# Mixers of a two-layer decoder: projection tiles cut into units between the small products, and another order of branch tiles

## The chip, the cores and the metric

The kernel runs on one core of a Trainium2 chip. The time is that of the device for one launch, in microseconds (us), the median of several executions. Engines are named as the profile does: PE (TensorE, matrix products), DVE (VectorE), ACT (ScalarE), POOL (GpSimd) and SP (SyncE, which issues most transfers). PE has a clock of two levels, 1.2 and 2.4 GHz; the profile shows the share that was granted.

## The reference, cut to what matters

One inference step of a decoder with two layers, on 288 tokens: a prompt of 256 and 8 sequences of 4 sampled tokens. What the change touches is the first part of each layer, the token mixers:

```
z = u @ w_in                     # u: normalised input, 288 x 1024
a = GLA(z[...]), b = RetNet(z[...]), c = gated DeltaNet(z[...]), d = Mamba-2 SSD(z[...])
br = stack(a, b, c, d)           # each 288 x 512
proj = einsum('blnv,nvd->blnd', br, w_branch)
gates = sigmoid(mg)              # mg: the last 4 x 1024 columns of z
out = sum(gates * proj, over n) @ w_out
```

DeltaNet and SSD first run a causal convolution of width 4 over their columns. DeltaNet (GDN) also inverts a triangular matrix of 128 x 128 per head and block, in seven doubling levels. After the mixers come a SwiGLU (layer 0) or experts (layer 1) and a gate with a per-layer embedding. The states of all mixers are outputs too.

## The kernel before

All weights come through one stream of tiles of 128 x 1024 floats (512 KB) into a ring of five slots (RING), in the order that `tile_table` writes down. A tile is one of:
- `z`: a block of 128 columns of the input projection, for one mixer n. GLA, RetNet and GDN have 12 each, SSD has 10.
- `mg`: a block of the gate columns; 8 for each mixer.
- `br`: two blocks of the branch projection of mixer n, for which the final output of that mixer is needed; 4 for each mixer.

`z` and `mg` tiles are *projection tiles*. They are computed in a split form: ACT rounds the tile to a high part (`high`, L1346), DVE subtracts to get the low part (`low`, L1688), and PE sums three products (high x high, high x low, low x high, L715 to L717) for each of the 8 blocks of 128 rows: 24 products of 288 columns. The split tiles lie in three buffers (HELD), so the split of a tile waits until the tile three before it is done. A projection tile's ring slot is free when its low part is made. A *branch tile* isn't split: PE reads it from the ring (L762, 2 x 4 products, 16 records in the trace), and its slot is free when PE is done. SP waits for exactly these events, in the order of the stream, before it issues the transfer into a slot (`plain`, L677).

PE writes tile t to bank t % 2 (a branch tile to both). ACT takes a projection tile out of its bank: a `z` tile is copied to memory (L1374, L1375, L1378), an `mg` tile goes through a tanh (L1370). DVE takes a branch tile (`branch_tile`): (tanh + 1) times the product, for each of two banks (L1712), and from the second mixer on it is added to the sum (L1715). Before a tile is written, PE waits in `bank_is_free` until the tile that had the bank was taken.

The mixers run one after the other: `gla`, `ret`, `gdn`, `ssd`. Their own products are small and wait for each other through DVE, ACT and POOL. To fill PE, each mixer's order of work has numbered slots, and `SLOTS[n]` says how many tiles of the stream are issued in each; `fill(L, n, s)` issues them. The same call stands in ACT's and DVE's programs: ACT takes the tiles of the slot and makes the high parts that fall due (`highs`), DVE makes the low parts (`lows`) and takes the branch tiles. So the slots also set what ACT and DVE do ahead of and behind the mixer's own work. Each engine runs its own list in order. While mixer n runs, `z` tiles of mixer n + 1, `mg` tiles and the `br` tiles of mixer n - 1 are issued.

Places in a mixer that matter here:
- `core`: scores (L785), and for two heads at a time `outputs`: three products a head (L891 to L893), and for each of 8 sequences one product per head with the state as weights and 4 columns (L896).
- `out_sums` (L926, L929) behind a wait for ACT's squares, and `states` (L946, L950, L954), which waits for the masks that POOL makes.
- GDN and SSD start with `conv`: for each block of channels DVE makes four operations (L1908 to L1914), ACT a tanh (L1484), DVE two operations that finish it (L1896, L1898), and both fill one slot with it. On ACT the slot comes ahead of the tanh; on DVE it comes behind the finish. PE doesn't wait between slots 0 to 4.
- behind it GDN normalises queries and keys (reciprocal L2026, products L2028, L2029), then come the transposes (L842, L847) and the decays of the heads (L861 to L864).
- in GDN's inversion a level is 8 products (16 records, L1062), a copy by ACT (L1536), 16 products (L1069, L1071) and two subtractions by DVE (L2074, L2075), on which the next level waits.

Of the kernel before, what the change touches and what calls it, by code (L numbers as in the profile page):

```python
# [23 lines left out]
P = 128  # L24
# [4 lines left out]
TOK = SEQ + SAMP  # L29
# [165 lines left out]
def tile_table():  # L195

    out = []
    for L in range(DEPTH):
        def z(n):
            return [("z", L, n, b) for b in range(ZBLOCKS[n])]  # L200

        def mg(n):
            return [("mg", L, n, b) for b in range(KD)]

        def br(n):
            return [("br", L, n, b) for b in range(4)]

        out += z(0)
        out += z(1) + mg(0)
        out += br(0) + z(2) + mg(1)  # L210
        out += br(1) + z(3) + mg(2)
        out += br(2) + mg(3)
        out += br(3)
        out += [("out", L, 0, b) for b in range(KD)]
        if L % 2 == 0:
            for b in range(NF):
                out += [("gate", L, 0, b), ("up", L, 0, b)]
            out += [("down", L, 0, b) for b in range(NF)]
# [36 lines left out]
def tile_at(j, m, i):  # L255
# [1 line left out]
    return 2 * FIRST[j] + m * GROUPS[j] + i  # L257

SLOTS = [
# [5 lines left out]
]  # L265
NSLOT = [len(x) for x in SLOTS]


def fill_tiles(L):
    out = []  # L270
    for n in range(4):
        mine = [x for x in PLAIN if x[1] == L and ((x[0] == "z" and x[2] == n + 1) or (x[0] == "mg" and x[2] == n) or
                                                  (x[0] == "br" and x[2] == n - 1))]
# [30 lines left out]
def build(nc, io):  # L304
    ctx = ExitStack()
    with ctx:
# [391 lines left out]
        def _(pe):  # L698
            mm = nc.tensor.matmul

            def weights(x):
# [2 lines left out]
                pe.wait_ge(slot_in[t % RING], 16 * (t // RING + 1))  # L704
                return [ring[:, (t % RING) * TILE + P * i:(t % RING) * TILE + P * i + P] for i in range(8)]

            def product(out, x, uh, ul, norm_k=None):

                t = T_OF[x]
                q = Q_OF[t]  # L710
                pe.wait_ge(tile_low, q + 1)
                hi, lo = [[y[:, q % HELD, P * i:P * i + P] for i in range(KD)] for y in (t_high, t_low)]
                if norm_k is None:
                    for k in range(KD):
                        mm(out, hi[k], uh[:, k, :], start=k == 0, stop=False)  # L715
                        mm(out, hi[k], ul[:, k, :], start=False, stop=False)  # L716
                        last = mm(out, lo[k], uh[:, k, :], start=False, stop=k == KD - 1)  # L717
                    return last
                for k in range(KD):
# [18 lines left out]
            def stream_tile(x):  # L738
# [29 lines left out]
                            last = mm(bank(M + o)[:, 0:TOK], w[2 * o + k], ple_in[:, k, :], start=k == 0, stop=k == 1)  # L768
                last.then_inc(tile_done, 1)

            def fill(L, n, s):
                for x in FILL[L][n][s]:
                    stream_tile(x)

            def norm(k):
                for i in range(KD):
# [12 lines left out]
            def prep(L):  # L789
                pe.wait_ge(small_in[L], 16 * 5)  # L790
                for k in range(KD):
                    mm(bank(M)[0:16, 0:TOK], wsm[:, k, 0:16], u[:, k, :], start=k == 0, stop=k == KD - 1)
                for b, (t0, nt) in enumerate(TB):
                    for k in range(KD):
                        last = mm(bank(M + 1)[0:nt, 16 * b:16 * b + 16], u[:, k, t0:t0 + nt], wsm[:, k, 16:32],
                                  start=k == 0, stop=k == KD - 1)
                last.then_inc(small_ps, 1)
                pe.wait_ge(glr_ready, L + 1)
                for b, (t0, nt) in enumerate(TB):
                    last = mm(bank(M + 2 + b // 2)[0:nt, 256 * (b % 2):256 * (b % 2) + 256],  # L800
                              glrt[0:17, t0:t0 + nt], wgk[0:17, :], start=True, stop=True)
                last.then_inc(gk_ps, 1)
                for b in range(4, ZBLOCKS[0]):
                    stream_tile(("z", L, 0, b))
                pe.wait_ge(logd_ready, L + 1)

# [62 lines left out]
            def core(L, n, slot):  # L869
# [3 lines left out]
                def outputs(h0):  # L873
# [20 lines left out]
                    for b in range(NSEQ):  # L894
                        for i, (kr, pair, o, p, v) in enumerate(two):
                            last = mm(o[:, 256 + 4 * b:260 + 4 * b], st_of(n)[kr, pair, b, :],  # L896
                                      qg[kr, pair, 4 * b:4 * b + 4], start=False, stop=True, skip_group_check=True)
                            if b == NSEQ - 1:
                                last.then_inc(o_ps, 1)

                for hh in range(HEADS[n]):
                    gh = L * NHEAD + HBASE[n] + hh
                    if n != GLA:
                        kT, qT = qk_of(n, hh)
                        if hh < 2:
# [8 lines left out]
                        outputs(hh - 1)  # L914
                    fill(L, n, slot + hh)
                if n != GLA:
                    outputs(HEADS[n] - 2)

            def out_sums(L, n):
# [12 lines left out]
            def states(L, n):  # L932

                m, dv = 4 * L + n, DV[n]
                pe.wait_ge(ort_ready, m + 1)
                pe.wait_ge(o_taken, L * NHEAD + HBASE[n] + HEADS[n])
                for h0 in range(0, HEADS[n], 2):
                    gh = L * NHEAD + HBASE[n] + h0
                    two = []
# [12 lines left out]
                    for b in range(NSEQ):  # L952
                        for r, pair, kc, v, mk in two:
                            last = mm(bank(M + 2 * pair + b // 4)[r, dv * (b % 4):dv * (b % 4) + dv],  # L954
                                      mk[:, 64 * b:64 * b + 64], v[0:32, 2], start=True, stop=True)
                            if b == NSEQ - 1:
                                last.then_inc(masked_used, 1)

            def gla(L):
                m = 4 * L  # L960
# [41 lines left out]
                fill(L, GLA, 15)  # L1002
                out_sums(L, GLA)
                fill(L, GLA, 16)
                states(L, GLA)
                fill(L, GLA, 17)

            def gdn(L):
# [48 lines left out]
                for lv in range(7):  # L1057
# [4 lines left out]
                        last = mm(bank(M + g // 4)[:, 128 * (g % 4):128 * (g % 4) + 128], msk[:, g // 2, g % 2, :],  # L1062
                                  xm[:, g // 2, g % 2, :], start=True, stop=True)
                    last.then_inc(p_ps, 1)
                    fill(L, GDN, 16 + 2 * lv)
                    pe.wait_ge(p_ready, 7 * L + lv + 1)
                    for g in range(8):
                        c = slice(128 * (g % 4), 128 * (g % 4) + 128)
# [11 lines left out]
                last.then_inc(vn0_ps, 1)  # L1080
                pe.wait_ge(kbg_ready, L + 1)
                pe.wait_ge(state_in, 16 * (4 * L + GDN + 1))
                for b in range(NSEQ):
                    for hh in range(4):
                        r = slice(64 * (hh % 2), 64 * (hh % 2) + 64)
                        last = mm(bank(M + 1 + 4 * (hh % 2))[:, 32 * (hh // 2) + 4 * b:32 * (hh // 2) + 4 * b + 4], st_of(GDN)[r, hh // 2, b, :],
# [25 lines left out]
                fill(L, GDN, 37)  # L1112
                out_sums(L, GDN)
                fill(L, GDN, 38)
                states(L, GDN)
                for s in range(39, NSLOT[GDN]):
                    fill(L, GDN, s)

            def ret(L):
# [11 lines left out]
                fill(L, RET, 6)  # L1131
                out_sums(L, RET)
                fill(L, RET, 7)
                states(L, RET)
                for s in range(8, NSLOT[RET]):
                    fill(L, RET, s)

# [1463 lines left out]
```

## Time and profile before

| | |
|---|---|
| median of 3 runs | 2736.98 us (2736.95 to 2749.7) |
| profiled execution | 2750.4 us |
| its span, first to last instruction | 2748.3 us |
| mean granted clock of PE | 0.914 |
| busy share of the span | PE 90%, PE weight loads 77%, DVE 59%, ACT 39%, POOL 7% |
| mixers of layer 0 from GLA's transposes to the last branch tile | 82.9 to 714.1 us |
| the same of layer 1 | 1090.6 to 1707.4 us |

Busy shares are those of one execution. A product's duration in the rows is longer than the step from one start to the next, since products overlap in the array; for a run of products the steps count. A granted clock of 1.0 is the full level and 0.5 the half one, and a figure between is a mean over time. "idle before <-releaser" is how long the engine stood still ahead of the instruction, and the instruction of which engine let it go.

### The profile page before, as it was taken

The page shows a single profiled execution, that of the slowest core. Times are in us where ns is not written, and L with a number is a line of the kernel's source. Part 1 is how long each engine was busy: PE and PEld are TensorE (multiplying, and loading weights), DVE is VectorE, ACT ScalarE, POOL GpSimd, SP SyncE. Part 2 cuts the span into 40 slices and gives each one's busy share as a digit, 9 for nine tenths or more (in the row PEclk, how much of TensorE's full clock was granted, in tenths as well). Part 3 has the DMA queues.
Part 4 walks back from the last instruction along what each step waited for, and adds up shares of the span by engine and source line. Part 5 has one row for each costly group of instructions (what it writes and reads, how often), then busy time and mean ns, then how long its engine had stood idle before and what let it go on. Part 6 is the DMA issues. An engine that isn't in the chain of part 4 may idle for free.

```text
span 2748.3 us, 38217 instructions
## 1 busy us (share of the span) xinstructions
PE 2462.7 (90%) x14436; PEld 2124.5 (77%) x14436; DVE 1628.5 (59%) x2112; ACT 1074.4 (39%) x1450; POOL 178.8 (7%) x247
## 2 busy tenths in 40 slices
PE   8899868868999989889778879899999999999996
PEld 7788758857699978779678766678878778787786
DVE  4453554264366463544553443387887878778785
ACT  3322321112033343324221121166766667567563
POOL 0210101111000000211011201000000000000000
PEclk8889879778899999999889688799999999999999
DMA  5224321021345432323311122288988889889871
GB/s 192 93 82 141 117 74 50 31 97 39 137 146 166 164 129 93 105 103 115 125 54 47 59 70 72 90 309 301 333 294 317 303 300 331 294 299 321 299 282 74
DMA packets 122566, 456.43 MB, mean 166 GB/s; under 512 B 14056, under 2 KB 14474, under 8 KB 120018
## 3 DMA queue, kind: packets, MB, share of 16 engines
q1 hardware_dynamic: 118818, 432.66, 44.6%
q0 software_dynamic: 3632, 22.12, 2.2%
q8 instruction: 86, 1.41, 0.2%
q14 instruction: 30, 0.25, 0.0%
HBM read 443.72 MB, written 11.00 MB: 165 GB/s over the span
## 4 chain that ended last, share of the span: by engine, by line
PE 77%; DVE 11%; issue 5%; ACT 4%; DMA 1%; POOL 1%; DVEq 0%; SPq 0%; ACTq 0%; POOLq 0%
PE ps L715 9%; PE ps L717 8%; PE ps L716 8%; PE ps L762 5%; DVE weights_low L2220 4%; PE ps L1265 4%; PE ps L1267 3%; PE ps L1266 3%; PE ps L1287 3%; PE ps L1288 3%; PE ps L1289 3%; PE ps L1238 3%; PE ps L756 2%; PE ps L896 2%; DMA ring<-in_stream 1%
## 5 line engine op out<-in xcount | busy, mean ns | idle before, releaser
L715 PE MATMUL ps<-u_high,tiles_high 128*128 128x288 f32 x1688 | 535.1, 317 | 2.6 <-DVE arena L1712 2.6
L716 PE MATMUL ps<-u_low,tiles_high 128*128 128x288 f32 x1688 | 521.3, 309 | 0.0
L717 PE MATMUL ps<-u_high,tiles_low 128*128 128x288 f32 x1688 | 519.1, 307 | 0.0
L1688 DVE TENSOR_TENSOR tiles_low<-ring,tiles_high 128x1024 fp32r<-128x1024 f32 x238 | 291.7, 1229 | 268.7 <-ACT tiles_high L1346 267.6
L715 PEld LDWEIGHTS ps<-u_high,tiles_high 128*128 128x128 f32 x1688 | 340.8, 202 | 12.7 <-issue 6.7
L1346 ACT ACTIVATE tiles_high<-ring 128x1024 fp32r<-128x1024 f32 x238 | 250.7, 1054 | 245.9 <-DMA ring<-in_stream 155.9
L716 PEld LDWEIGHTS ps<-u_low,tiles_high 128*128 128x128 f32 x1688 | 341.0, 202 | 0.6
L717 PEld LDWEIGHTS ps<-u_high,tiles_low 128*128 128x128 f32 x1688 | 340.3, 202 | 0.0
L2220 DVE TENSOR_TENSOR weights_low<-expert_ring,weights_high 128x1024 fp32r<-128x1024 f32 x288 | 334.3, 1217 | 4.9 <-ACT weights_high L1597 2.2
L1265 PE MATMUL ps<-weights_high,u_high 128*128 128x512 f32 (+1 forms) x768 | 297.6, 388 | 23.2 <-DVE weights_low L2220 22.6
L2220 DVE TENSOR_TENSOR weights_low<-ring,weights_high 128x1024 fp32r<-128x1024 f32 x240 | 280.1, 1217 | 42.9 <-ACT weights_high L1597 41.8
L1597 ACT ACTIVATE weights_high<-expert_ring 128x1024 fp32r<-128x1024 f32 x288 | 283.3, 1052 | 27.4 <-PE ps L1267 27.4
L1267 PE MATMUL ps<-weights_high,u_low 128*128 128x512 f32 (+1 forms) x768 | 289.1, 376 | 0.0
L1266 PE MATMUL ps<-weights_low,u_high 128*128 128x512 f32 (+1 forms) x768 | 289.0, 376 | 0.0
L1597 ACT ACTIVATE weights_high<-ring 128x1024 fp32r<-128x1024 f32 x240 | 236.4, 1052 | 78.9 <-PE ps L1289 42.2
L762 PE MATMUL ps<-arena,ring 128*128 128x288 f32 x512 | 155.9, 470 | 64.2 <-DVE arena L1712 59.6
L762 PEld LDWEIGHTS ps<-arena,ring 128*128 128x128 f32 x512 | 113.2, 224 | 106.7 <-issue 71.7
L1265 PEld LDWEIGHTS ps<-weights_high,u_high 128*128 128x128 f32 x768 | 144.5, 188 | 59.9 <-DVE weights_low L2220 38.1
L1267 PEld LDWEIGHTS ps<-weights_high,u_low 128*128 128x128 f32 x768 | 144.5, 188 | 23.4
L1266 PEld LDWEIGHTS ps<-weights_low,u_high 128*128 128x128 f32 x768 | 144.8, 188 | 21.7
L1287 PE MATMUL ps<-weights_high,tiles_high 128*128 128x512 f32 x352 | 141.1, 401 | 0.0
L1288 PE MATMUL ps<-weights_low,tiles_high 128*128 128x512 f32 x352 | 139.5, 396 | 0.0
(381 smaller groups left out, 3377.6 us busy)
## 6 DMA issues: line engine op xcount, KB each, us to landing
ring<-in_stream SPq DMA_DIRECT2D x530, 512.0 KB, 4.2
expert_ring<-in_stream SPq DMA_DIRECT2D x288, 512.0 KB, 5.5
arena<-in_state POOLq DMA_DIRECT2D x8, 1024.0 KB, 5.2
state_s<-arena POOLq DMA_DIRECT2D x8, 1024.0 KB, 4.2
const<-in_const SPq DMA_DIRECT2D x1, 2052.5 KB, 12.0
arena<-in_const POOLq DMA_DIRECT2D x2, 832.0 KB, 4.9
h<-in_x SPq DMA_DIRECT2D x1, 1152.0 KB, 5.1
y<-acc POOLq DMA_DIRECT2D x1, 1152.0 KB, 4.4
```

Of the source, the lines that this page charges most:

```text
L715: mm(out, hi[k], uh[:, k, :], start=k == 0, stop=False)
L716: mm(out, hi[k], ul[:, k, :], start=False, stop=False)
L717: last = mm(out, lo[k], uh[:, k, :], start=False, stop=k == KD - 1)
L762: last = mm(bank(o)[:, 0:TOK], w[4 * o + k], src, start=k == 0, stop=k == 3)
L1265: mm(out, xg_high[:, k, :], hi, start=k == 0, stop=False)
L1266: mm(out, xg_high[:, k, :], lo, start=False, stop=False)
L1267: last = mm(out, xg_low[:, k, :], hi, start=False, stop=k == KD - 1)
L1287: mm(out, e_high[:, f, :], hi, start=f == 0, stop=False)
L1346: A(t_high[:, q % HELD, :], ring[:, (t % RING) * TILE:(t % RING + 1) * TILE], ACT.Copy).then_inc(tile_high, 1)
L1597: A(w_high[:, o // 4, o % 4].rearrange("p k c -> p (k c)"), expert_slot(t), ACT.Copy).then_inc(w_high_ready, 1)
L1688: tt(t_low[:, q % HELD, :], ring[:, (t % RING) * TILE:(t % RING + 1) * TILE], t_high[:, q % HELD, :].bitcast(F32), ALU.subtract).then_inc( ...
L2220: tt(lo, expert_slot(t), hi.bitcast(F32), ALU.subtract).then_inc(w_low_ready, 1)
```

## The change

1. `tile_table` has another order: with mixer n's slots no longer go `br` of n - 1, `z` of n + 1 and `mg` of n. The gate tiles of mixer 1 move from RetNet's slots to the start of GDN's, ahead of `br(1)`; those of mixer 2 from GDN's slots to the start of SSD's, ahead of `br(2)`. `MG_STAGE` says which mixer's slots take which gate tiles. RetNet's slots hold 16 tiles instead of 24, GDN's 22 as before, SSD's 20 instead of 12.
2. `SLOTS` is written anew. In GDN's slots 0 to 5, ahead of and in the convolutions, stand the eight gate tiles, in 6 and 7 a branch tile each, in 13 and 17 one each, and then one `z` tile in each level of the inversion from the second on (slots 19 to 29), in 35 and in 37 to 39. In SSD's slots 0 to 7 stands a gate tile each, in 9 to 12 (between the decays of pairs of heads) a branch tile each, and gate tiles in 13, 15, 17, 19, two in 21 and two in 22.
3. On PE a tile can be issued in units: three products of a projection tile, or one product of a branch tile. `begin` waits for the bank and makes the tile the current one, `drip` issues some of its units, and `fill` first issues what is left of it and then the other tiles of the slot. Units stand:
   - in `prep` between the small projections for the token-major gates (L795), with the tile `z` 4 that stood behind the next products before
   - in `outputs`, one unit behind the products of each of the 8 sequences
   - in `states` of GLA, RetNet and GDN, one for every second sequence
   - in GDN's inversion, three units between the first and the second group of products of a level
4. On ACT and DVE only the order of tiles changes, through the tables.

```diff
-        out += br(0) + z(2) + mg(1)
-        out += br(1) + z(3) + mg(2)
-        out += br(2) + mg(3)
+        out += br(0) + z(2)
+        out += mg(1) + br(1) + z(3)
+        out += mg(2) + br(2) + mg(3)
...
 SLOTS = [
-    [2, 2, 2, 1, 1, 1, 1, 0, 1, 0, 1, 1, 1, 1, 1, 1, 1, 2],
-    [3, 2, 2, 3, 3, 2, 2, 2, 2, 3],
-    [1, 0, 1, 1, 0, 1, 0, 2, 0, 1, 0, 0, 2, 1, 0, 1, 0, 1, 0, 1, 0, 1, 0, 1, 0, 1, 1, 0, 0, 0, 1,
-     1, 0, 0, 0, 0, 0, 1, 1, 1, 0],
-    [0, 1, 1, 2, 1, 0, 1, 0, 0, 1, 0, 0, 0, 0, 0, 0, 0, 1, 0, 1, 0, 2, 1],
+    [3, 1, 2, 1, 1, 1, 1, 0, 1, 0, 1, 1, 1, 1, 1, 1, 1, 2],
+    [2, 1, 1, 1, 2, 1, 2, 2, 2, 2],
+    [1, 1, 2, 1, 2, 1, 1, 1, 0, 0, 0, 0, 0, 1, 0, 0] + [0, 1] * 7 + [0, 0, 0, 0, 0, 1, 0, 1, 1, 1, 0],
+    [1, 1, 1, 1, 1, 1, 1, 1, 0, 1, 1, 1, 1, 1, 0, 1, 0, 1, 0, 1, 0, 2, 2],
 ]
+MG_STAGE = [0, 2, 3, 3]
...
+            def product_units(out, x):
+                q = Q_OF[T_OF[x]]
+                pe.wait_ge(tile_low, q + 1)
+                for k in range(KD):
+                    hi, lo = [y[:, q % HELD, P * k:P * k + P] for y in (t_high, t_low)]
+                    mm(out, hi, u_high[:, k, :], start=k == 0, stop=False)
+                    mm(out, hi, u_low[:, k, :], start=False, stop=False)
+                    last = mm(out, lo, u_high[:, k, :], start=False, stop=k == KD - 1)
+                    if k == KD - 1:
+                        last.then_inc(tile_done, 1)
+                    yield
...
+                def begin(self, x):
+                    self.tile = x
+                    t = T_OF[x]
+                    if x[0] == "br":
+                        self.units = branch_units(x)
+                    else:
+                        bank_is_free(t, t % 2)
+                        self.units = product_units(bank(t % 2)[:, 0:TOK], x)
+                def drip(self, count):
+                    for _ in range(count if self.units else 0):
+                        next(self.units, None)
+                def finish(self):
+                    self.drip(9)
+                    done, self.tile, self.units = self.tile, None, None
+                    return done
...
             def fill(L, n, s):
+                begun = tiles.finish()
                 for x in FILL[L][n][s]:
-                    stream_tile(x)
+                    if x != begun:
+                        stream_tile(x)
... in prep
+                tiles.begin(("z", L, 0, 4))
                 for b, (t0, nt) in enumerate(TB):
                     for k in range(KD):
...
+                        if k % 3 == 2:
+                            tiles.drip(1)
+                tiles.finish()
                 pe.wait_ge(glr_ready, L + 1)
... in outputs, behind the two heads' products of a sequence
+                        tiles.drip(1)
... in core
                 for hh in range(HEADS[n]):
+                    begin(L, n, slot + hh)
...
                 if n != GLA:
+                    begin(L, n, slot + HEADS[n])
                     outputs(HEADS[n] - 2)
... in states (slots 17, 39 and 8 of GLA, GDN and RetNet; none for SSD)
+                if slot is not None:
+                    begin(L, n, slot)
...
+                        if b % 2:
+                            tiles.drip(1)
... in the inversion
                     last.then_inc(p_ps, 1)
-                    fill(L, GDN, 16 + 2 * lv)
+                    begin(L, GDN, 17 + 2 * lv)
+                    tiles.drip(3)
                     pe.wait_ge(p_ready, 7 * L + lv + 1)
```

## Rows read from the trace of the kernel before

**Rows 1.** Page, busy us, share of the span and instructions of each engine.
```profile
PE 2462.7 (90%) x14436; PEld 2124.5 (77%) x14436; DVE 1628.5 (59%) x2112; ACT 1074.4 (39%) x1450; POOL 178.8 (7%) x247
```

**Rows 2.** Stretches: window, us, busy by engine, granted clock, DMA share, GB/s.
```profile
210.40:328.50 118.10, 110.00 (x773) 100.88 (x772) 56.24 (x57) 35.15 (x57) 16.89 (x35) 0.94 0.40 135
328.50:388.20 59.70, 30.38 (x121) 23.29 (x119) 35.92 (x59) 14.49 (x22) 0.00 (x0) 0.73 0.20 71
388.20:431.50 43.30, 40.98 (x258) 36.79 (x259) 20.15 (x43) 8.79 (x23) 4.84 (x7) 0.78 0.18 61
431.50:503.40 71.90, 60.28 (x482) 58.78 (x480) 28.33 (x26) 16.64 (x21) 11.04 (x13) 0.98 0.13 45
503.40:569.40 66.00, 62.28 (x421) 56.88 (x422) 27.12 (x28) 10.86 (x16) 10.10 (x8) 0.69 0.09 29
569.40:613.00 43.60, 24.39 (x88) 18.21 (x86) 23.30 (x48) 6.92 (x12) 3.55 (x14) 0.77 0.35 127
613.00:634.00 21.00, 17.83 (x111) 15.67 (x111) 14.72 (x43) 8.04 (x21) 3.08 (x2) 1.00 0.19 65
634.00:696.10 62.10, 55.89 (x364) 39.71 (x364) 21.53 (x30) 12.71 (x20) 10.81 (x10) 0.76 0.08 26
```

**Rows 3.** Stretches again: the mixers of layer 0 and of layer 1.
```profile
82.90:714.10 631.20, 535.00 (x3533) 467.79 (x3533) 298.74 (x419) 150.60 (x252) 86.15 (x116) 0.84 0.24 81
...
1090.60:1707.40 616.80, 521.86 (x3533) 456.38 (x3533) 298.81 (x419) 151.90 (x253) 86.42 (x116) 0.86 0.24 82
```

**Rows 4.** PE's waits in layer 0's mixers: us in total, times, longest.
```profile
PE ps L762 <- DVE arena L1712: 30.5, 4, 9.3
PE ps L842 <- DVE arena L2029: 13.9, 1, 13.9
PE ps L1069 <- ACT arena L1536: 6.7, 6, 1.1
...
PE ps L1062 <- DVE arena L2075: 2.5, 1, 2.5
```

**Rows 5.** Timeline of GDN's convolutions: start, us, instruction, [idle before, releaser].
```profile
328.37 4.04 PE L762 MATMUL ps<-arena,ring 128*128 128x288 f32 x16
339.54 7.11 PE L762 MATMUL ps<-arena,ring 128*128 128x288 f32 x16 [7.13 <-DVE arena L1712]
...
349.92 1.06 ACT L1346 ACTIVATE tiles_high<-ring 128x1024 fp32r<-128x1024 f32 x1 [12.37 <-DMA ring<-in_stream]
...
351.36 0.42 DVE L1896 SCALAR_TENSOR_TENSOR arena<-arena 128x256 f32<-128x256 f32 x1 [5.95 <-ACT arena L1484]
...
353.66 6.88 PE L762 MATMUL ps<-arena,ring 128*128 128x288 f32 x16 [7.01 <-DVE arena L1712]
...
355.18 0.55 DVE L1910 SCALAR_TENSOR_TENSOR arena<-arena,pv 128x312 f32<-128x312 f32 x1
...
379.36 7.35 DVE L2026 RECIPROCAL arena<-arena 128x1152 f32<-128x1152 f32 x1
```

**Rows 6.** Timeline of PE: products in a row, at the half and the full level.
```profile
48.29 0.44 PE L715 MATMUL ps<-u_high,tiles_high 128*128 128x288 f32 x1
48.53 0.44 PE L716 MATMUL ps<-u_low,tiles_high 128*128 128x288 f32 x1
...
286.07 0.30 PE L716 MATMUL ps<-u_low,tiles_high 128*128 128x288 f32 x1
286.20 0.29 PE L717 MATMUL ps<-u_high,tiles_low 128*128 128x288 f32 x1
```

**Rows 7.** Page, the costliest groups: DVE's split of a tile.
```profile
L1688 DVE TENSOR_TENSOR tiles_low<-ring,tiles_high 128x1024 fp32r<-128x1024 f32 x238 | 291.7, 1229 | 268.7 <-ACT tiles_high L1346 267.6
```

**Rows 8.** Timeline of PE: around one pair of RetNet's outputs.
```profile
281.69 0.59 PE L891 MATMUL ps<-arena 128*128 128x256 f32 x2
...
282.76 0.70 PE L891 MATMUL ps<-arena 128*128 128x256 f32 x2
...
285.83 0.40 PE L715 MATMUL ps<-u_high,tiles_high 128*128 128x288 f32 x1
```

More of the change, by code:

```diff
@@ L271, in fill_tiles @@
     for n in range(4):
-        mine = [x for x in PLAIN if x[1] == L and ((x[0] == "z" and x[2] == n + 1) or (x[0] == "mg" and x[2] == n) or
+        mine = [x for x in PLAIN if x[1] == L and ((x[0] == "z" and x[2] == n + 1) or (x[0] == "mg" and MG_STAGE[x[2]] == n) or
                                                   (x[0] == "br" and x[2] == n - 1))]
@@ L705, in weights, with branch_units, __init__ @@
                 return [ring[:, (t % RING) * TILE + P * i:(t % RING) * TILE + P * i + P] for i in range(8)]
+            def product_units(out, x):
[9 more added lines that the diff above has]
+                    yield
+            def branch_units(x):
+                t = T_OF[x]
+                _, L, n, b = x
+                pe.wait_ge(o_final, 4 * L + n + 1)
+                w = weights(x)
+                for o in range(2):
+                    bank_is_free(t, o)
+                    for k in range(4):
+                        last = mm(bank(o)[:, 0:TOK], w[4 * o + k], zblk(n, OUT0[n] + k)[:, 0:TOK], start=k == 0, stop=k == 3)
+                        if k == 3:
+                            last.then_inc((branch_ps, tile_done)[o], 1)
+                        yield
+            class Fill:
+                def __init__(self):
+                    self.tile = self.units = None
+                def begin(self, x):
+                    self.tile = x
+                    t = T_OF[x]
+                    if x[0] == "br":
[10 more added lines that the diff above has]
+                    return done
+            tiles = Fill()
             def product(out, x, uh, ul, norm_k=None):
@@ L769, in stream_tile, with begin @@
                 last.then_inc(tile_done, 1)
+            def begin(L, n, s):
+                if FILL[L][n][s]:
+                    tiles.begin(FILL[L][n][s][0])
             def fill(L, n, s):
+                begun = tiles.finish()
                 for x in FILL[L][n][s]:
-                    stream_tile(x)
+                    if x != begun:
+                        stream_tile(x)
             def norm(k):
@@ L796, in prep @@
                                   start=k == 0, stop=k == KD - 1)
-                last.then_inc(small_ps, 1)
+                        if (b, k) == (2, KD - 1):
+                            last.then_inc(small_ps, 1)
+                        if k % 3 == 2:
+                            tiles.drip(1)
+                tiles.finish()
                 pe.wait_ge(glr_ready, L + 1)
@@ L802, in prep @@
                 last.then_inc(gk_ps, 1)
-                for b in range(4, ZBLOCKS[0]):
+                for b in range(5, ZBLOCKS[0]):
                     stream_tile(("z", L, 0, b))
@@ L930, in out_sums, with states @@
                 last.then_inc(osum_ps, 1)
-            def states(L, n):
+            def states(L, n, slot=None):
                 m, dv = 4 * L + n, DV[n]
@@ L1004, in gla @@
                 fill(L, GLA, 16)
-                states(L, GLA)
+                states(L, GLA, 17)
                 fill(L, GLA, 17)
@@ L1082, in gdn @@
                 pe.wait_ge(state_in, 16 * (4 * L + GDN + 1))
+                begin(L, GDN, 30)
                 for b in range(NSEQ):
+                    tiles.drip(1)
                     for hh in range(4):
@@ L1114, in gdn @@
                 fill(L, GDN, 38)
-                states(L, GDN)
+                states(L, GDN, 39)
                 for s in range(39, NSLOT[GDN]):
@@ L1133, in ret @@
                 fill(L, RET, 7)
-                states(L, RET)
+                states(L, RET, 8)
                 for s in range(8, NSLOT[RET]):
```

## The prediction

> **What bounds the kernel now.** I read the page's busy rows first. TensorE (PE) is busy in 90% of the span [rows 1], so only what shortens PE's own work or fills its idle time counts. Then the stages of the four mixers of layer 0, cut where PE's work changes [rows 2]: RetNet is full (110.0 of 118.1 us), the two stretches in which VectorE (DVE) computes the short convolutions are half empty (30.4 of 59.7 and 24.4 of 43.6), and the stretches with many small products are full but run at a granted clock of 0.69 to 0.78. Layer 1 repeats this: the same stages take 616.8 us against 631.2, with the same instruction count and a clock of 0.86 and 0.84 [rows 3]. I work out one layer and double it; everything outside the mixers is taken as it is. The waits of PE say why the convolution stretches are empty [rows 4]: branch products (L762) wait 30.5 us for DVE to take the branch before (L1712), one transpose waits 13.9 us for the normalised keys (L2029), and in the delta rule's inversion (GDN) six products wait 1.1 us each for ScalarE's (ACT) copy, the last level 2.5 us for DVE's subtraction.
>
> How the long wait comes about is in the timeline of one convolution step [rows 5]. A branch product ends near 346.65 (339.54 + 7.11). Its slot in the ring is then free, the next transfer lands, and ACT, which waited 12.37 us for it, splits that tile at 349.92. Only after that does ACT compute the tanh of the convolution, on which DVE waits 5.95 us until 351.36, and only behind that does DVE take the branch, so that PE's next branch product starts at 353.66. One such turn takes 14.1 us for 4.0 us of products.
>
> **The units of work.** A projection tile is 24 products. At the full level (2.4 GHz) they start 0.133 us apart, 3.2 us a tile; at the half level (1.2 GHz) 0.24 us apart, 5.8 us [rows 6]. A branch tile is 16 records, 4.04 us at the full level and 7.1 at the half [rows 5].
>
> **The change, part by part, in one layer.** Both orders issue 46 projection and 12 branch tiles from RetNet's start on. No product, split or transfer is added or lost; DVE's 1.23 us [rows 7] and ACT's 1.06 us [rows 5] per split go with the tile.
>
> 1. *RetNet, 118.1 us.* Eight gate tiles leave a stretch that PE fills: 8 x 3.2 = -25.6. Its own chain (scores, sums, states) still has 12 tiles beside it, and PE's only waits there are a few us.
> 2. *GDN's convolutions, 59.7 us.* Before: 2 projection and 4 branch tiles. After: 8 and 2. Six of the eight conv steps now turn on projection tiles, whose slot is free once they are split, so ACT doesn't wait for a transfer. Eight tiles 25.6, the sums 2.1, some 7 for splits that DVE reaches late (a conv block is 4 operations of at most 0.55, some 2.1 us, [rows 5]), a branch tile 4.0, the wait for its taking 7.1, the second at the half level 7.1. Then the tail: transfer 3.3 (346.65 to 349.92), split 1.1, tanh, finish, split, branch taking (some 5, a sum of neighbouring rows, my estimate), reciprocal 7.35, two products 1.5. Together 71 to 73: +13. Ends: 54 (-6) if nothing waits beside the tail, 88 (+28) if every tile costs half a turn.
> 3. *To the inversion, 43.3 us.* Five projection tiles leave, one branch tile comes: -16.0 + 4.0; decays and the small inverse then wait some 2 us openly. -10 (ends -13, -5).
> 4. *Inversion, 71.9 us.* Nine products (1.2 us) now stand in the 1.1 us for which PE waits on ACT, and fifteen (2.0) behind the second group. They were the cover of DVE's subtraction, which needs 2.5 us [rows 4]: 0.5 us becomes open per level. Six times -1.1 + 0.5, the last level 2.5 to 0.5: -5.5 (ends -8, 0). One branch tile more fits in.
> 5. *GDN's outputs and states, 66.0 us at 0.69.* That clock means 62% of it, 41 us, at the half level, where a product takes 0.24 instead of 0.133: 18 us lost. The weights products with 4 columns (L896) alone precede such drops. With three 288-column products between every few of them I expect a third back, -6, not all, as the waits ahead of the outputs stay. One tile fewer -3.2; the tile that hid ACT's taking and square now stands ahead of them, +3 of open wait: about -7 (ends -21, +3).
> 6. *SSD's convolutions, 43.6 us.* Four branch tiles go, six projection tiles come. The pace is then DVE's block: 2.1 + finish 0.6 + split 1.2 = 3.9, six times, and 2.6 at the start: 26. -17.5 (ends -20, 0).
> 7. *SSD's transposes and decays, 21.0 us.* Four branch tiles come between the pairs of heads, 16.2 us of products. Each must be taken by DVE (two products and a sum, some 1.6) behind a split that waits for a transfer, but the decay products of the next pair lie beside. +13 (ends +8; +45 if each costs the whole turn of 14.1, less the 11 us of decays beside them).
> 8. *SSD's core, sums and states, 62.1 us at 0.76.* Three tiles more, +9.6; 48% at the half level costs 13 us, of which I count 7 back; the wait for y before the sums grows by 3: +6 (ends -1, +13).
> 9. *The switching.* A projection product behind a small one starts 0.24 instead of 0.133 us ahead of its follower (285.83, 286.07, 286.20 [rows 6, 8]); a small pair behind a projection product takes 0.59 instead of 0.70 [rows 8]. Net some 0.08 us a unit (ends 0 and 0.18), in some 94 units: +7.
> 10. *Start of the layer and GLA.* Three tiles in GLA's first slot look as if they fill its wait (L974), but DVE must first split for the third, which waits for the tile before it, so the wait moves along: 0. The tile among the small projections runs earlier, but its bank is only read by ACT after the logarithms, so the tile that reuses the bank waits: -1. GLA's two cores win the clock in one layer and lose the cover of the square (2 us): 0.
>
> The wait for a free bank now stands ahead of small products, with outputs and states queued behind it on PE, and ACT and DVE after them. It is for a tile two before, which ACT has taken by then in its own order, so I cost it at nothing; if ACT were late, the outputs would start late by one tile, 3.2.
>
> Sum: -25.6 + 13 - 10 - 5.5 - 7 - 17.5 + 13 + 6 + 7 - 1 = -27.6 us a layer, -55 in both. The profiled execution took 2750.4 us (span 2748.3), so it would take 2695; the median before is 2736.98, 13.4 lower, and by it the forecast is **2682 us**.
>
> **A rule against it.** The rows first: over both layers' mixers the granted clock is 0.84 and 0.86 [rows 3], so some 30% of 1248 us pass at the half level, and I count 13 us a layer of that back. "TensorE: Matmul & The Clock Gate" of the Trainium skill (What's actually happening) says that the ramp is under 1% of a typical kernel's span. By it less than 27 us could be won from the clock in all, and the bounds of steps 5 and 8 would lose their lower ends. This trace doesn't agree for this kernel.
> A second one (Step-by-step: what each phase is for, same page) is that PE pulls the next weight load ahead under a running product. By it the switching of step 9 would be a gain rather than a cost. The row on the small pair agrees (0.59 against 0.70), the row on the product behind it does not.
>
> **The rivals.**
> *The clock holds.* If small and large products mixed keep PE at the full level in steps 3, 5 and 8, 19 + 41 + 30 us at the half level end, worth 0.45 each: 40 us instead of the 13 counted. -27 more a layer: 2628. For it: the inversion, products without long pauses, runs at 0.98 [rows 2]. Against: the waits ahead of each core remain.
> *Moved, not hidden.* The convolution stretches may not be held by branch tiles but by the alternation ACT, DVE, PE, which projection tiles need too (take, split, tanh, finish, split). Then step 6 gives nothing (+17.5) and step 2 costs 5 more: +45 in both layers, 2727. For it: every convolution step waits for ACT (5.95). Against: the 12.37 us are a wait for a transfer that only branch slots cause.
> *The turn goes with the branch tile (slower).* Six branch tiles of a layer now stand in GDN's slots 13 and 17 and between SSD's decays. If each drags ACT and DVE through the turn of 14.1 us, step 7 costs 32 more and the two others 10 each: +52 a layer, 2786. It decides, that is over 2751, from 5.8 us more per tile. For it: the same transfer wait stands in ACT's queue ahead of the decays' exponentials. Against: four of them have other PE work beside, and no convolution waits.
>
> **How the numbers follow.** Forecast (2650 to 2713) 0.63, clock 0.12, moved 0.15, slower 0.10. Under 0.5%, 13.7 us, this kernel can't be told from unchanged. Faster: 0.63 + 0.12 and a third of the third case, 0.80; same 0.10; slower 0.10. The range leaves out the far half of the first rival and the slower one: 2640 to 2732.
>
> **What would show it.** L762's wait for L1712 falls from 30 us to some 10 a layer (2, 6). RetNet's stretch is near 92 us; L842's wait for L2029 grows to about 18 (2). L1069's wait for L1536 is gone and L1062 waits 0.5 per level (4). SSD's convolutions take about 26 us, its decays about 25 to 34 with transposes (6, 7). A clock over 0.9 in the output stretches would say that I took too little from it; a split (L1346) waiting over 5 us for a transfer between SSD's decays that I took too little for step 7. Wrong altogether if the two layers' mixers together are not shorter by 30 to 80 us.

## The result, and the profile after

The changed kernel takes 2807.64 us (median of 4 runs, 2802.55 to 2808.91) against 2736.97 beside it: the ratio is 1.024, with an interval of 1.021 to 1.027. It is slower by 2.4%, where 2682 was forecast. Its profiled execution took 2806.45 us, with a span of 2804.7 and a mean granted clock of 0.908. Two of kernel 4's ten executions below, at 3961 and 7926 us, were disturbed, and its 2742.7 is the median of the other eight.

The page's busy rows of the changed kernel, against [rows 1]:

```profile
PE 2540.4 (91%) x14436; PEld 2145.0 (76%) x14436; DVE 1631.4 (58%) x2112; ACT 1071.8 (38%) x1450; POOL 178.9 (6%) x247
```

DVE and ACT do the same work. PE, with the same 14436 records, is busy 78 us longer: the loss is inside PE's own work, not in waits. The stretches of layer 0 in the changed kernel, cut at the same events as [rows 2] (window, us, busy of PE, PEld, DVE, ACT, POOL, granted clock, DMA share, GB/s), and then the mixers of both layers, against [rows 3]:

```profile
211.30:320.40 109.10, 98.84 (x578) 82.64 (x577) 43.61 (x44) 24.67 (x42) 15.17 (x32) 0.84 0.30 107
320.40:395.60 75.20, 42.74 (x237) 37.88 (x235) 41.62 (x66) 21.47 (x31) 0.62 (x4) 0.79 0.22 77
395.60:434.10 38.50, 31.30 (x154) 23.84 (x154) 18.28 (x43) 3.25 (x11) 4.83 (x7) 0.68 0.04 14
434.10:503.40 69.30, 65.96 (x496) 62.28 (x496) 27.65 (x29) 14.61 (x24) 9.99 (x13) 0.96 0.17 62
503.40:580.50 77.10, 70.15 (x396) 55.65 (x397) 25.61 (x26) 11.05 (x17) 10.09 (x6) 0.64 0.09 28
580.50:605.80 25.30, 21.41 (x145) 20.35 (x144) 23.88 (x43) 11.94 (x20) 5.99 (x16) 0.95 0.60 202
605.80:640.80 35.00, 33.23 (x175) 27.73 (x175) 23.75 (x58) 8.78 (x22) 2.05 (x2) 1.00 0.25 78
640.80:714.60 73.80, 66.51 (x436) 47.03 (x436) 22.33 (x32) 16.78 (x26) 10.78 (x10) 0.89 0.18 63
83.60:733.80 650.20, 562.91 (x3533) 469.67 (x3533) 301.36 (x421) 149.32 (x252) 86.66 (x116) 0.84 0.23 78
1108.40:1764.00 655.60, 570.70 (x3533) 474.85 (x3533) 300.42 (x421) 150.85 (x254) 86.00 (x116) 0.84 0.23 78
```

RetNet gave up eight tiles, 25.6 us of products, and is only 9 us shorter at a clock of 0.84 (0.94 before). GDN's outputs and states are 11 us longer, not 7 shorter. Both layers' mixers together are 57.8 us longer (19.0 and 38.8), where the forecast had called itself wrong altogether unless they were 30 to 80 shorter. SSD's convolutions (25.3) and its transposes with decays (35.0) are where the forecast put them (26 and 34).

PE's waits in layer 0 of the changed kernel, against [rows 4]. L818 is the branch product, L911 the transposes, L998 SSD's sums behind ACT's squares, L713 a unit's product, L1138 the inversion's first products:

```profile
PE ps L911 <- DVE arena L2108: 18.3, 1, 18.3
...
PE ps L818 <- DVE arena L1791: 7.2, 1, 7.2
PE ps L998 <- ACT arena L1534: 5.6, 1, 5.6
...
PE ps L713 <- DVE tiles_low L1767: 3.2, 1, 3.2
...
PE ps L1138 <- DVE arena L2154: 2.7, 5, 0.5
```

The waits went as forecast: branch products 30.5 to 7.2, the keys 18.3, the inversion's six waits for ACT's copy gone, 0.5 open per level. And yet the layer is longer.

What a unit costs is in PE's timeline of the changed kernel, in RetNet's outputs of layer 1 at the full level and in GDN's outputs of layer 0 at the half one. L965 x4 are the four small products of a sequence, with 4 columns each, L713 to L715 the unit:

```profile
1274.41 0.39 PE L965 MATMUL ps<-arena 64*128 64x4 f32 x4
1274.73 0.40 PE L713 MATMUL ps<-u_high,tiles_high 128*128 128x288 f32 x1
1274.97 0.29 PE L714 MATMUL ps<-u_low,tiles_high 128*128 128x288 f32 x1
1275.10 0.29 PE L715 MATMUL ps<-u_high,tiles_low 128*128 128x288 f32 x1
1275.32 0.39 PE L965 MATMUL ps<-arena 64*128 64x4 f32 x4
...
532.04 0.61 PE L713 MATMUL ps<-u_high,tiles_high 128*128 128x288 f32 x1
...
533.58 0.61 PE L713 MATMUL ps<-u_high,tiles_high 128*128 128x288 f32 x1
```

A cycle of four small records and a unit takes 0.91 us at the full level (1274.41 to 1275.32) and 1.54 at the half (532.04 to 533.58). The same work unmixed stands in the third kernel below (new order, units in the inversion alone):

```profile
252.05 1.95 PE L965 MATMUL ps<-arena 64*128 64x4 f32 x32
253.93 0.40 PE L772 MATMUL ps<-u_high,tiles_high 128*128 128x288 f32 x1
...
501.61 3.58 PE L965 MATMUL ps<-arena 64*128 64x4 f32 x32
505.12 0.61 PE L772 MATMUL ps<-u_high,tiles_high 128*128 128x288 f32 x1
```

32 small records take 1.88 us from start to start, 0.235 for four, or 3.51 and 0.44 at the half level; a unit in a row of products takes 0.40 or 0.72 [rows 6]. So a unit between small products costs 0.91 - 0.64 = 0.27 us at the full level, and 1.54 - 1.16 = 0.38 at the half. The forecast had 0.08. SSD's products on 64 rows and 64 columns pay the same: the cycle is 0.81 (660.07 to 660.88), four of them unmixed take 0.13 (kernel 3, 32 from 623.48 to 624.51), which leaves 0.28.

```profile
660.07 0.28 PE L965 MATMUL ps<-arena 64*64 64x4 f32 x4
...
660.88 0.28 PE L965 MATMUL ps<-arena 64*64 64x4 f32 x4
```
```profile
623.48 1.10 PE L965 MATMUL ps<-arena 64*64 64x4 f32 x32
624.51 0.40 PE L772 MATMUL ps<-u_high,tiles_high 128*128 128x288 f32 x1
```

### The profile page after: what moved, and what is told of

Read it like the earlier page. It is cut to its first block, busy times and chain, and to the rows that moved or that the text cites. A ratio compares the mean times of both kernels' runs of the same rounds, so it can differ in the third digit from the quotient of the medians.

```text
span 2804.7 us, 38220 instructions
## 1 busy us (share of the span) xinstructions
PE 2540.4 (91%) x14436; PEld 2145.0 (76%) x14436; DVE 1631.4 (58%) x2112; ACT 1071.8 (38%) x1450; POOL 178.9 (6%) x247
## 4 chain that ended last, share of the span: by engine, by line
PE 75%; DVE 13%; issue 5%; ACT 4%; POOL 1%; DMA 1%; DVEq 0%; SPq 0%; ACTq 0%; POOLq 0%
PE ps L771 5%; PE ps L773 5%; PE ps L772 5%; PE ps L818 4%; DVE weights_low L2299 4%; PE ps L1344 4%; PE ps L713 3%; PE ps L1346 3%; PE ps L1345 3%; PE ps L1366 3%; PE ps L1367 3%; PE ps L1368 3%; PE ps L1317 3%; PE ps L812 2%; PE ps L965 2%
## 5 line engine op out<-in xcount | busy, mean ns | idle before, releaser
L771 PE MATMUL ps<-u_high,tiles_high 128*128 128x288 f32 x1288 | 401.6, 312 | 20.3 <-DVE tiles_low L1767 17.1
L772 PE MATMUL ps<-u_low,tiles_high 128*128 128x288 f32 x1288 | 393.4, 305 | 0.0
L773 PE MATMUL ps<-u_high,tiles_low 128*128 128x288 f32 x1288 | 391.6, 304 | 0.0
L1676 ACT ACTIVATE weights_high<-expert_ring 128x1024 fp32r<-128x1024 f32 x288 | 283.3, 1051 | 27.6 <-PE ps L1346 27.6
L771 PEld LDWEIGHTS ps<-u_high,tiles_high 128*128 128x128 f32 x1288 | 256.3, 199 | 31.3 <-issue 23.6
L772 PEld LDWEIGHTS ps<-u_low,tiles_high 128*128 128x128 f32 x1288 | 255.9, 199 | 0.7
L773 PEld LDWEIGHTS ps<-u_high,tiles_low 128*128 128x128 f32 x1288 | 255.4, 198 | 0.0
L713 PE MATMUL ps<-u_high,tiles_high 128*128 128x288 f32 x400 | 158.5, 396 | 6.3 <-DVE tiles_low L1767 6.3
L1368 PE MATMUL ps<-weights_high,tiles_low 128*128 128x512 f32 x352 | 139.5, 396 | 0.0
```

The lines of the kernel that those rows point to most:

```text
L713: mm(out, hi, u_high[:, k, :], start=k == 0, stop=False)
L1676: A(w_high[:, o // 4, o % 4].rearrange("p k c -> p (k c)"), expert_slot(t), ACT.Copy).then_inc(w_high_ready, 1)
```

## The experiments

| kernel | us | ratio to before, interval |
|---|---|---|
| changed | 2807.6 | 1.021 to 1.027 |
| 1 new order, no units | 2705.5 | 0.980 to 0.991 |
| 2 old order, all units | 2855.1 | 1.037 to 1.047 |
| 3 new order, units in the inversion | 2701.4 | 0.979 to 0.989 |
| 4 all units but those of the outputs | 2742.7 | 0.997 to 1.003 |
| 5 small products on all rows | 2814.9 | 1.024 to 1.030 |
| 6 lumps of four units | 2720.2 | 0.992 to 0.996 |
| 7 old order, units in the inversion | 2728.5 | 0.994 to 0.998 |
| 8 as 3, branch tiles of GDN later | 2650.1 | 0.964 to 0.969 |
| 9 as 8, gate tiles left in place | 2642.9 | 0.965 to 0.970 |
| 10 changed kernel with the slots of 8 | 2761.1 | 1.007 to 1.011 |
| 11 as 8, one gate tile later too | 2640.3 | 0.964 to 0.967 |
| 12 as 8, lumps in GLA and GDN | 2654.4 | 0.969 to 0.972 |

**1 to 4: units or order.** `MIX` says where `begin` acts; where it doesn't, the tile is issued whole in its slot.

```
+MIX = ()                # 2: all places, and the old tile_table and SLOTS; 3: ("inv",); 4: all but "out"
-                if FILL[L][n][s]:
+                if where in MIX and FILL[L][n][s]:
```

> The new order and slots, with every tile issued whole in its slot as before the change. Theory A (the units cost): the traces of before and after show one cycle of small products and a unit at the full level in 0.91 us, against 0.64 for the same work unmixed, +0.27 us; some 110 units a layer stand among small products, 59 us in both layers, and the stretches of outputs stay at the half level with them. So without units the time is 2807 - 59 = 2748, down to 2720 if the clock comes back too. Theory B (the order costs: gate tiles put into the convolutions, branch tiles between SSD's decays): the time stays at 2790 or more.

> The old order and slots (one tile of the inversion moved by half a level, from slot 26 to 27), with units in all the places of the change. Theory A: 2737 + 59 for switching, less some 5 to 10 for the inversion, more if the clock stays low: 2785 to 2815. Theory B: within 10 us of 2737.

> The new order, with units in the inversion alone. Theory A: 3 to 5 us a layer under the new order alone (forecast step 4 gave 5.5, the stretch of the changed kernel showed 2.7 to 3.6): 2712 to 2742. Theory B: 2785 or more.

> The changed kernel without the units in the four outputs (80 of 110 a layer); those in the start, in the states and in the inversion stay. Theory A: 2807 - 160 x 0.27 = 2764, down to 2745 if the clock comes back in the outputs. Theory B: 2795 or more.

Theory A (the units cost) holds and B (the order costs) falls: without units the new order is 1.5% faster than before, and units under the old order alone cost 117 us (the old slots put 64 of them a layer in the outputs instead of 80, and 8 among GDN's products of keys and states). The units cost more than the expectations had: kernels 1 and 3 came out below their ranges, kernel 2 above. From kernel 3 to the changed one 106 us are lost in 2 x 110 units outside the inversion, 0.48 each: 65 in the 160 units of the outputs, 41 in the other 60. Kernel 3's whole tiles follow such small products 13 times a layer and pay a change there too, so 194 changes were added, not 220; at 0.27 to 0.38 each they explain 52 to 74.

SSD's core shows the change almost alone, as its clock hardly moves: the stretch in kernel 3, in the changed kernel, and in kernel 6 below.

```profile
601.70:640.50 38.80, 35.96 (x333) 31.60 (x333) 15.49 (x26) 11.07 (x19) 4.66 (x4) 0.96 0.25 92
```
```profile
640.80:689.00 48.20, 42.59 (x332) 33.21 (x332) 15.52 (x26) 10.91 (x18) 4.64 (x4) 0.96 0.20 74
```
```profile
611.20:652.90 41.70, 37.19 (x332) 32.12 (x332) 15.51 (x27) 10.96 (x18) 4.65 (x4) 0.94 0.24 87
```

PE goes 4, 32 and 8 times from 4-column products to a projection product there: 9.4 us for 28 times more (0.34 each), 6.5 us back for 24 fewer (0.27).

Elsewhere the clock and waits come on top. They show in RetNet's sums and states of layer 1, the same 162 records of PE in both kernels: the window of kernel 3, that of kernel 4, and PE's timeline of kernel 4 inside it:

```profile
1242.30:1265.80 23.50, 20.81 (x162) 19.31 (x161) 16.39 (x8) 6.75 (x11) 4.28 (x4) 0.78 0.33 118
```
```profile
1262.70:1293.40 30.70, 26.05 (x162) 20.40 (x161) 12.28 (x7) 6.75 (x11) 2.04 (x2) 0.72 0.21 69
```
```profile
1271.89 0.65 PE L1029 MATMUL ps<-arena 32*64 32x128 f32 x8
1277.11 0.61 PE L714 MATMUL ps<-u_high,tiles_high 128*128 128x288 f32 x1 [4.57 <-DVE tiles_low L1768]
1277.52 0.44 PE L715 MATMUL ps<-u_low,tiles_high 128*128 128x288 f32 x1
```

The mixed order takes 7.2 us more for eight units. The first unit waits 4.57 us for DVE's split, with the states queued behind it (kernel 3 waits 2.7 there, for POOL's masks). Behind the pause PE is at the half level (a product lasts 0.44, as in [rows 6]) and stays there until the last unit; in kernel 3 the same products stand in one row behind the states.

**5: why a switch costs.** SSD's small products are 64 x 64, RetNet's 64 x 128, and both pay 0.27 to 0.28, so half the columns of the array make no difference here.

```
-                        two.append((slice(64 * half, 64 * half + 64), pair,
+                        two.append((slice(64 * half, 64 * half + 64) if n == SSD else slice(0, P), pair,
```

> The changed kernel, where the small products of GLA's, RetNet's and GDN's outputs use all 128 rows of the array instead of 64 (the sum then runs over two heads' rows, so these outputs are not the reference's; SSD's stay as they are). A cycle of four small records and a unit takes 0.907 us in the changed kernel, 0.27 more than unmixed. Theory A1 (the price comes from changing the shape of the tile in the array, 64 rows against 128): the cycle falls to 0.64 to 0.70, and the time by some 96 x 0.25 = 24 us to 2785. Theory A2 (any change between a small and a projection product costs this): the cycle stays at 0.88 or more, the time at 2800 to 2815.

The cycle fell to 0.84 or 0.85 at the full level, between the two theories, and the time did not fall (2814.9). What happened is in the weight loads: RetNet's outputs in the changed kernel (L965), and the same in this one (L966).

```profile
1274.97 0.19 PEld L715 LDWEIGHTS ps<-u_high,tiles_low 128*128 128x128 f32 x1
1275.32 0.30 PEld L965 LDWEIGHTS ps<-arena 64*128 64x128 f32 x4 [0.16 <-issue]
```
```profile
1277.46 0.19 PEld L716 LDWEIGHTS ps<-u_high,tiles_low 128*128 128x128 f32 x1
1277.59 0.54 PEld L966 LDWEIGHTS ps<-arena 128*128 128x128 f32 x4
```

On all rows the small load starts 0.13 us behind the load before it, while the last large product runs, and the cycle has nothing left over: 0.40 for the unit and four loads at 0.11 are 0.84. On 64 rows the load starts 0.35 us behind, only with its own product. So the loads speak for A1's mechanism, and its number was missed: I had let the small records keep the 0.06 that they take on 64 rows, while on all rows they take 0.11. At the half level nothing is won: the cycle is 1.57 (below) against 1.54.

```profile
1280.28 0.59 PE L714 MATMUL ps<-u_high,tiles_high 128*128 128x288 f32 x1
...
1281.85 0.59 PE L714 MATMUL ps<-u_high,tiles_high 128*128 128x288 f32 x1
```

No run has these small products on all rows and unmixed. That 0.11 is their own price is read from the loads in the cycle alone, so the cause of the 0.27 is in this last step argued, not shown. "TensorEngine Tiling (Array Packing)" of the Trainium skill (Key Properties) says that a change of tiling mode drains the engine. The loads fit that, at 0.27 us for a change there and back.

**6: the number of switches.**

```
-                        tiles.drip(1)
+                        if b % 4 == 3:
+                            tiles.drip(4)       # in states: drip(2)
```

> The changed kernel with twelve products (four units) behind every fourth sequence of the outputs instead of three behind each, and six products behind every fourth in the states. The same work stands at the same places, with 32 switches a layer there instead of 104. Theory A (each switch costs 0.27): 2 x 72 x 0.27 = 39 us less, 2768, and lower if a longer run of products lets the clock rise. If the place of the tile costs, and not the number of switches (rival C: outputs finished later by a whole tile's time, 3.2 us each in 12 places a layer): it stays at 2795 or more.

2720: 87 us for 144 switches fewer, 0.6 each, with the same tiles in the same places. Rival C (the place of the tile costs) falls. That is more than the change itself, which SSD's core above has at 0.27. What the rest is stays open: the mean clock rose from 0.908 to 0.923, but of layer 0's stretches GLA went from 127.7 to 116.7 us at 0.88 and then 0.93, and GDN's outputs from 76.2 to 65.5 at an unchanged 0.64.

**7: the inversion alone.** Only `MIX = ("inv",)` with the old order (the tile of slot 26 in 27).

> The old order with units in the inversion alone. By step 4 of the forecast 5.5 us a layer (bounds 0 and 8): 2726. With both old order and units everywhere the inversion took 66.4 us against 71.8, 5.4 less, which says the same; under the new order, with a branch tile more in it, the gain was 3.7. Rival: the gain was noise of the clock, 2732 or more.

2728.5, and the inversion takes 66.4 us in both layers (71.9 before [rows 2]): 5.4, as step 4 said. Its products and the units both use all 128 rows. Over both layers that would be 11 us, and the time fell by 8.2.

**8 to 12: the order.** GDN's slots 0 to 15 in the changed kernel, and in kernels 8, 9 and 11 (10 and 12 have those of 8; 12 lets units into GLA's and GDN's outputs, with 6's edit):

```
-[1, 1, 2, 1, 2, 1, 1, 1, 0, 0, 0, 0, 0, 1, 0, 0]   # changed kernel
+[1, 1, 2, 1, 1, 1, 1, 0, 0, 1, 0, 0, 1, 1, 0, 0]   # 8
+[1, 1, 2, 1, 2, 1, 0, 0, 0, 1, 0, 0, 1, 1, 0, 0]   # 9
+[1, 1, 1, 1, 1, 1, 1, 0, 0, 1, 1, 0, 1, 1, 0, 0]   # 11
```

> The new order with units in the inversion alone (2701), with the tiles of GDN's slots 4 to 17 moved later: one gate tile from slot 4 to 5 and on to 6, and the two branch tiles of slots 6 and 7 to slots 9 and 12, behind the transposes. The stretch from GDN's transposes to the inversion runs at 0.63 there, at 0.86 in layer 1 of the kernel before, which had five projection tiles in it. Theory D (without tiles of its own this stretch falls to the half level): with two branch tiles more (8.1 us at the full level) it takes about as long as now, 41 us, at 0.8, while the convolutions lose a branch turn of 10: 2685. Rival: the small products set the clock there whatever stands between, and DVE is late with two more branch tiles: 2700 or more.

> As the kernel with the branch tiles moved later (2650), but all eight gate tiles stay in GDN's slots 0 to 5 (1, 1, 2, 1, 2, 1) and only the two branch tiles go from slots 6 and 7 to 9 and 12. Theory F (the two branch tiles in the last convolution steps cost a turn each, which the forecast priced at 4.0 + 7.1 + 7.1): nearly the whole gain stays, 2645 to 2660. Rival: the gain came from one gate tile less ahead of the fifth step, 2685 or more.

> The changed kernel with all its units, and only the slots of GDN's gate and branch tiles as in the kernel that took 2650. If the price of the units and that of the two branch tiles are independent: 2807 - 51 = 2756, within 8. If the two share their loss of clock: 2770 or more, or 2740 or less.

> As the kernel that took 2650, with gate tiles one in each slot 0 to 6 and the eighth in slot 9, behind the transposes, and the branch tiles in 10, 12, 13 and 17. VectorE sets the pace in the convolutions (PE waits 3.7 us for a split), so one split fewer there makes them 1.2 us shorter, the tile's 3.2 us of products go to a stretch at 0.88: between 2645 and 2655 if the tile only moves, 2640 or less if it also fills the small inverse's waits there (2.1 us a layer) and keeps the clock up.

> As the kernel that took 2650, with twelve products behind every fourth sequence in GLA's and GDN's outputs alone. In the kernel with such lumps everywhere GLA took 2 to 3 us a layer less and GDN's outputs 2.4 less in layer 1, 3.1 more in layer 0. Theory A (few switches cost little, and long runs of products raise the clock where it had fallen): 2640 to 2648. Rival: the difference was chance of the clock, 2648 to 2655.

Kernel 8 gave 51 us where 16 were expected. Kernel 9 shows that it was the two branch tiles (F; 58 us). Kernel 10 falls 46.5 under the changed one: the two prices are independent within some 5 us. Kernel 11 is 10 us under 8 and level with 9. The gain that kernel 6 had let me expect for 12 didn't come: it is 4 us slower than 8. DVE's and ACT's timeline in layer 0 of kernel 3, at the last convolution step, and then DVE's of kernel 9:

```profile
352.68 1.06 ACT L1425 ACTIVATE tiles_high<-ring 128x1024 fp32r<-128x1024 f32 x1 [8.92 <-DMA ring<-in_stream]
...
355.61 0.43 DVE L1975 SCALAR_TENSOR_TENSOR arena<-arena 128x256 f32<-128x256 f32 x1 [11.04 <-ACT arena L1563]
...
358.96 7.35 DVE L2105 RECIPROCAL arena<-arena 128x1152 f32<-128x1152 f32 x1
```
```profile
335.64 0.43 DVE L1975 SCALAR_TENSOR_TENSOR arena<-arena 128x256 f32<-128x256 f32 x1 [1.55 <-ACT arena L1563]
335.98 0.19 DVE L1977 SCALAR_TENSOR_TENSOR arena<-arena 128x32 f32<-128x32 f32 x1
336.20 7.35 DVE L2105 RECIPROCAL arena<-arena 128x1152 f32<-128x1152 f32 x1
```

Behind a branch tile ACT waits 8.92 us for the transfer into its slot, and the tanh stands behind that; with the branch tiles past the transposes DVE waits 1.55 for it instead of 11.04. The stretches of layer 0 from RetNet's start to the transposes, and from there to the inversion, in kernel 3 and then in kernel 9:

```profile
200.50:367.90 167.40, 127.08 (x812) 113.72 (x811) 86.51 (x108) 46.40 (x73) 16.27 (x34) 0.87 0.30 101
367.90:408.90 41.00, 33.77 (x155) 25.48 (x155) 18.32 (x42) 3.25 (x11) 4.85 (x7) 0.62 0.04 14
```
```profile
197.60:345.10 147.50, 116.57 (x781) 106.13 (x779) 80.93 (x100) 44.27 (x71) 16.71 (x35) 0.88 0.32 110
345.10:382.00 36.90, 31.64 (x186) 24.46 (x186) 22.77 (x50) 5.36 (x13) 5.21 (x7) 0.87 0.13 44
```

The two tiles leave 19.9 us behind, and where they go the stretch is 4.1 us shorter with 31 records more, for its clock rises from 0.62 to 0.87. These 24 us are not all: the mixers of layer 0 fell by 35.1 (605.4 to 570.3), of which 8.7 lie in GDN's outputs and states, where no slot was changed (61.8 us at 0.64, then 53.1 at 0.77), and 2.8 in GLA. Why the clock is higher there no run shows. Kernels 9 and 11 beat both kernels of this case, the one before by 3.3 and 3.5%.

## Why the prediction was wrong, step by step

- **Step 9, the switching, is the one that failed.** It allowed +7 a layer (0.08 us a unit, at most 0.18). From kernel 3 to the changed one it is 106 / 2 = 53 a layer. It counted the units at 94 instead of 110, and it got the price of one seam wrong. The way from small to large was read rightly: 0.11 more for the first projection product (0.24 instead of 0.13), then as now. The way from large to small was put down as a gain of 0.11 (0.59 against 0.70), read in [rows 8] from a 256-column product with the label 128*128, which has the shape of the projection products. The 4-column products have 64 rows. In front of them the last projection product takes 0.22 instead of 0.13 (1275.10 to 1275.32), and the four of them 0.32 instead of 0.235 (1274.41 to 1274.73): 0.17 lost, and the three parts make the 0.27 above. In the terms of the forecast's second rule, the weight load comes early between products of one shape (0.13 behind the load before it), and not between these shapes (0.35). The trace of the kernel before had the seam, in front of RetNet's scores on 64 rows:

```profile
240.46 0.29 PE L717 MATMUL ps<-u_high,tiles_low 128*128 128x288 f32 x1
240.68 1.09 PE L785 MATMUL ps<-arena 64*128 64x256 f32 x6
```

Its 0.22 from start to start would have shown that part of the price before any run.

- **Step 5's gain of clock** (a third back, -6; the step's terms add up to -6.2, not -7) did not come: GDN's outputs and states run at 0.64 with units against 0.63 to 0.64 without, and take 77.1 us (59 forecast; kernel 3: 61.8). Mixing didn't bring PE back to the full level.
- **Step 3** lost half of its gain in layer 0 and all of it in layer 1: five tiles left the stretch to the inversion, and the clock fell from 0.78 to 0.68 in the changed kernel, 0.62 in kernel 3. It took 38.5 us instead of 33.3, in layer 1 40.8 (39.6 before).
- **Steps 1 and 2** together: some 165 forecast (92.5 and 72 to 73), 167.4 in kernel 3. Right for the order, with the branch turns priced about right; the units put 17 us on top (184.3). What I didn't see is that the two turns needn't be paid.
- **Step 4**: 5.5 forecast, 5.4 in kernel 7, 3.7 from kernel 1 to 3 (71.8 to 68.1).
- **Steps 6 and 7**: 26 and 34 forecast, 25.3 and 35.0 measured.
- **Step 8**: 68.1 forecast, 66.3 in kernel 3 (38.8 and 27.5), whose core runs at 0.96 with four whole tiles: its clock came back without units, which then cost 7.5.
- **Step 10** put GLA at 0, but its units cost as well: in layer 1 it takes 128.5 us against 117.7 in kernel 3.

Of the rivals, *the turn goes with the branch tile* was near the time (2786) for the wrong reason: its turns between SSD's decays did not come (step 7), those in the convolutions were in the forecast. *Moved, not hidden* fell with step 6, *the clock holds* with step 5. There was no rival in which the units themselves cost, beyond the 0.18 that step 9 had as its end.

In sum, a layer was forecast at -27.6. The order with the inversion's units gives -27.4 and -15.3 in the two layers of kernel 3 (605.4 and 603.1 against 632.8 and 618.4). 8.6 of the 27.4 are luck: they lie in GLA, 118.9 us at a clock of 0.90 instead of 127.5 at 0.83, and kernel 1, with the same order there, has 127.5 at 0.83. 46 us a layer more than allowed went to the units. Not settled is how the 0.48 us a unit divides into switch, wait and clock: 0.27 to 0.38 is the switch at the two levels for the 4-column products, the rest is the other two together; nor was the unit among the 32-row products of the states, or in the start, priced by itself.

## What to carry to other kernels

Read the price of an interleaving from both seams, there and back, with the shapes that will meet: products that use another part of the array than the stream around them cost a sum at each visit (here 0.27 us for 0.64 of work), so mix in long runs, or only among products of the same shape (as in the inversion, kernel 7). When tiles are moved out of a stretch of small products, count the clock they kept up. And in this kernel a tile that needs a fresh transfer belonged behind the last step that another engine must do in order after it, not between such steps.

## What the hardware showed that I had not expected

- A switch there and back between 64-row and 128-row products costs 0.27 us at the full level and 0.38 at the half, and at the full level 64 x 64 and 64 x 128 cost the same. With 128 rows on both sides the cycle of 0.85 is no longer than its weight loads (0.40 + 4 x 0.11).
- A mixed stream doesn't hold the level that it enters with. RetNet's outputs of layer 1 in the changed kernel enter at the full level (cycles of 0.91) and fall to the half one inside the stream, without a wait:

```profile
1275.64 0.40 PE L713 MATMUL ps<-u_high,tiles_high 128*128 128x288 f32 x1
1276.45 0.59 PE L965 MATMUL ps<-arena 64*128 64x4 f32 x4
```

SSD's core keeps 0.96 and 0.99 in the changed kernel with its units, and ran at 0.54 with those of kernel 2 in layer 0. What decides between the levels no run shows.

- Two branch tiles (8 us) put into a stretch of 41 us of mostly small products and waits raise its clock from 0.62 to 0.87, and it gets shorter with them (41.0 to 36.9 us).
